# Overflow rounds moved ahead of the rounds of four, the last spread accumulated onto h in PSUM, and the final norm taken by token halves out of PSUM

## The chip, the cores and the metric

The kernel runs on one core of a Trainium2 chip. The metric is the device time of one execution in microseconds. Three executions of the kernel before took 942.13, 942.78 and 943.84 us; the median is 942.78.

## The reference

One layer of a streaming encoder over 512 tokens of width 1024, all float32. Two branches (a gMLP spatial gate and a sliding-window attention) are gated and merged onto the residual `h`. Then comes a mixture of 32 experts: each token picks one group of 8 experts and the two best in it. Last comes a norm of the sum:

```python
def hierarchical_moe(x, w_rg, b_rg, w_re, b_re, w_gate, w_up, w_down):
    ...
    for e in range(N_EXPERTS):
        h = jax.nn.silu(xf @ w_gate[e]) * (xf @ w_up[e])
        y = y + combine[:, e:e + 1] * (h @ w_down[e])
    ...
        h = h + hierarchical_moe(hn, ...)
    return rmsnorm(h, norm_final_g)
```

`w_gate` and `w_up` are 1024x512 per expert, `w_down` 512x1024: 6 MB an expert, 192 MB in all, each read once.

## The kernel before, in words

Up to about 450 us it computes the two branches and the router. The change touches only what follows, the expert stage and the end.

**Rounds.** The experts go through 14 rounds (`ITERS`). Rounds 0 to 11 take two experts each, with room for 64 tokens per expert. Rounds 12 and 13 take four each, the eight experts with the fewest tokens, with room for 32. Tokens that find no room go to overflow rounds, a loop at the end behind a branch on `n_over > 0`, on each of TensorE, ScalarE, VectorE and SyncE. With these inputs nothing overflows: no overflow round runs in the trace, and each engine jumps over the loop's body.

**A round on TensorE.** `project` gate into bank 0 (L734), `turn_weights` (L744: the rows' weights turned into bank 7), `project` up into bank 1, half 0 of the spread of the round before (L797, L798), `turn_rows` (L751), half 1 of that spread, `project_down` into banks 5 and 6 (L766). For the last round `project_last_down` (L782) takes the down weights in three parts as they land. The fp32 weights of two or four experts stand in column tiles of 64 or 32 of the array. `spread` multiplies a one-hot matrix with `y_hi` and `y_lo`, and brings each row of y to its token: eight sums of 128x512, one for each of four token tiles and two halves. Ahead of each even round `gather_rows` (L718) picks the tokens' rows of the normed h for two rounds, 64 matmuls, with a one-hot that VectorE makes in `make_onehot` (L1379 to L1395), and `copy_pack` moves them to SBUF.

**A round on the other engines.** ScalarE: silu, the copy of the turned rows (`actT`), `y_hi` (L1006). VectorE: `row_weights`, in odd rounds `make_onehot` for the next two, `act_on_rows` (L1472), `add_rows` of the round before (L1491: eight adds of a sum in PSUM onto `h_tok`), `low_y` (L1480). So a round's spread and adds lie inside the next round.

**The weights.** SyncE issues them in order (L351). A step is one matrix of two experts, 4 MB, issued as two DMAs of 2 MB. There are four slots of SBUF, and step k waits until TensorE has finished the projection of step k-4. In numbers: rounds 0 to 11 are steps 0 to 35. Round 12 has gate 36 and 37, up 38 and 39, down 40 and 41; round 13 has 42 to 47. So steps 40 and 41 are issued when gate 12 is done, 42 and 43 when up 12 is, 44 and 45 when down 12 is, 46 and 47 when gate 13 is. Step 47 comes in three parts (L419), and behind it `final_g` (L424).

**The end.** `spread` of round 13, `add_rows`, then each engine loads the count `n_over` and branches. VectorE takes bn statistics of token tiles 2 and 3, ScalarE squares of tiles 0 and 1, GpSimd multiplies tiles 2 and 3 with `final_g` (L472). VectorE computes the root for all four (`inverse_root`: Newton steps on 128x4 elements) and finishes tiles 0 and 1 (L1540), ScalarE scales tiles 2 and 3 (L1030), and SyncE stores four tiles of 512 KB (L438). Semaphores tie all this together; there is no planner, the order is that of the code of each engine.

Of the kernel before, what the change touches and what calls it, by code (L numbers as in the profile page):

```python
# [7 lines left out]
F32 = mybir.dt.float32  # L8
# [7 lines left out]
P = 128  # L16
# [6 lines left out]
def build_block(nc, x, norm_mix_g, w_in, gate_bias, gmlp_ln_g, gmlp_ln_b, gmlp_w_s, gmlp_b_s,  # L23
# [28 lines left out]
    LIGHT_ROWS = ROWS // 2  # L52
    HEAVY = SORTED - LIGHT
    ITERS = FIXED // 2 + HEAVY // 2 + LIGHT // 4
    OV_ROW = ITERS * P
    assert ITERS % 2 == OV_PAIRS % 4 == 0
# [72 lines left out]
    result = at("result", [P, TT, D], F32, 32)  # L129

# [47 lines left out]
    with ctx:  # L178
# [57 lines left out]
        for c in range(UNITS):  # L236
# [33 lines left out]
        row_step, onehot_ready = sem("row_step"), sem("onehot_ready")  # L270
        pack_done, pack_a, pack_b = sem("pack_done"), sem("pack_a"), sem("pack_b")
        gate_done, up_done, silu_ready, rows_ready, rows_turned, actT_ready = (
            sem(n) for n in ("gate_done", "up_done", "silu_ready", "rows_ready", "rows_turned", "actT_ready"))
        y_left, down_done, y_hi_ready, y_lo_ready = (sem(n) for n in ("y_left", "down_done", "y_hi_ready", "y_lo_ready"))
        weights_turned, row_weight_ready, onehotT_ready = (
            sem(n) for n in ("weights_turned", "row_weight_ready", "onehotT_ready"))
        spread_done, h_added = sem("spread_done"), sem("h_added")
        ysq_summed, final_gained, out_stored = sem("ysq_summed"), sem("final_gained"), sem("out_stored")
        y_rstd_ready = sem("y_rstd_ready")
# [4 lines left out]
        h_final = sem("h_final")  # L284
# [21 lines left out]
        SPREAD_BANKS = ((2, 3, 5, 6), (7, 0, 1, 2))  # L306


        def experts_of(i):
            return 4 if i >= (FIXED + HEAVY) // 2 else 2  # L310

# [12 lines left out]
        def over_slot(j, q, m):  # L324

            slot = (3 * q + m) % 4
            before = STEPS_DONE // 4 - (1 if slot == LAST_SLOT else 0)
            return [(slot, 32 * (before + 3 * j + (3 * q + m) // 4) + (64 if slot == 0 else 32))]
# [11 lines left out]
        def _(sp):  # L340
# [7 lines left out]
            def load_step(slot, w, e0, e1):  # L348

                for s, e in enumerate((e0, e1)):  # L350
                    sp.dma_start(R[2 * slot + s][:, :].rearrange("p (a n) -> p a n", a=1),  # L351
                                 w[0, bass.ds(e, 1), :, :].rearrange("a (p c) n -> p a (c n)", p=P)
                                 ).then_inc(slot_loaded[slot], 16)
# [34 lines left out]
            DONE = (gate_done, up_done, down_done)  # L388
            for i in range(1, ITERS):
                n_e, r = experts_of(i), 2 * i - FIXED  # L390
                if i < FIXED // 2:
# [7 lines left out]
                for m, w in enumerate((w_gate, w_up, w_down)):  # L399
                    if i == 1 and m == 0:  # L400
                        continue
                    for a in range(n_e // 2):
                        k = step_at[i, m, a]
                        i4, m4, _ = steps[k - 4]
                        if k == 4:
                            for half, done in enumerate((gate_half_done, gate_done)):
# [16 lines left out]
            sp.wait_ge(routed, 1)  # L423
            sp.dma_start(final_g[:, :], norm_final_g.partition_broadcast(P)).then_inc(late_loaded, 16)  # L424
            n_over = sp.value_load(ov_count[0:1, 0:1], min_val=0, max_val=OV_TILES)

            with sp.If(n_over > 0):
                with sp.Fori(0, OV_PAIRS // 4) as j:
                    for q in range(4):
                        k = 4 * j + q  # L430
                        e0 = sp.value_load(ov_expert[0:1, bass.ds(2 * k, 1)], min_val=0, max_val=NE - 1)
                        e1 = sp.value_load(ov_expert[0:1, bass.ds(2 * k + 1, 1)], min_val=0, max_val=NE - 1)
                        sp.wait_ge(down_done, 4 * j + ITERS + q)
                        for m, w in enumerate((w_gate, w_up, w_down)):
                            load_step((3 * q + m) % 4, w, e0, e1)
# [7 lines left out]
        def _(pool):  # L443
# [32 lines left out]
        def _(pe):  # L476
# [220 lines left out]
            def gather_first():  # L697

                for part, ready in ((hn_hi, hn_hi_ready), (hn_lo, hn_lo_ready)):
                    for t in range(TT):  # L700
# [3 lines left out]
                        for c in range(KT):  # L704
# [4 lines left out]
                            if last and c % 2 == 1:  # L709
                                mm.then_inc(pack_done, 1)  # L710

            def gather_rows(g):

                pe.wait_ge(onehot_ready, g)
                for c in range(KT):
# [5 lines left out]
                    if c % 2 == 1:  # L721
                        mm.then_inc(pack_done, 1)

            def project(slots, odd, dst, done, packed=None, half_done=None):

                for slot, loaded in slots:
                    pe.wait_ge(slot_loaded[slot], loaded)
                n_e = 2 * len(slots)
                w = P // n_e
                for c in range(KT):  # L730
                    if packed is not None and c % 2 == 0:
                        pe.wait_ge(pack_b if c // 2 % 2 else pack_a, packed + c // 4)
# [8 lines left out]
            def turn_weights(odd):  # L741
# [3 lines left out]
                mm.then_inc(weights_turned, 1)  # L745

            def turn_rows(i):

                pe.wait_ge(rows_ready, i + 1)
                for c in range(FT):  # L750
                    mm = pe.transpose(bank[4][:, c * P:(c + 1) * P], act_rows[:, c, :], ident[:, :])  # L751
                mm.then_inc(rows_turned, 1)

            def project_down(slots, i, added):

                pe.wait_ge(actT_ready, i + 1)
                for slot, loaded in slots:
                    pe.wait_ge(slot_loaded[slot], loaded)
# [806 lines left out]
```

## Time and profile before

| | us |
|---|---|
| median of three executions | 942.78 |
| profiled execution | 942.76 |
| its span | 941.0 |
| TensorE busy in the span | 860.6 |
| VectorE busy | 438.5 |
| ScalarE busy | 211.2 |
| GpSimd busy | 8.4 |

All times below are counted from the start of the span. Section 2 of the page cuts the span into 40 slices of 23.5 us; a digit is the busy share of a slice in tenths. A TensorE matmul in fp32 appears as two records in the trace, one of the rounded fp32 form as one. "idle before" in a timeline is the engine's idle time ahead of the row, and behind the arrow stands what ended it.

### The profile page before, as it was taken

The numbers are of one execution on the slowest core, as the hardware profiler recorded it, in microseconds if no ns is written. First come the engines' busy times: TensorE is split into PE (matmuls) and PEld (weight loads), VectorE is DVE, ScalarE is ACT, GpSimd is POOL, SyncE is SP. The second block draws the span as 40 slices with busy tenths as digits, with TensorE's granted clock in tenths as the row PEclk, the third lists the DMA queues.
The fourth block names the chain that finished last, engine by engine and source line by source line (L and its number), as shares of the span: only waits on it lengthen the run. The fifth ranks groups of instructions, "written<-read, shape, count | busy, mean of one in ns | idle before, by whom it ended". The sixth has DMA issues, their size and how long they took to land.

```text
span 941.0 us, 11130 instructions
## 1 busy us (share of the span) xinstructions
PE 860.6 (91%) x4569; PEld 558.1 (59%) x4569; DVE 438.5 (47%) x811; ACT 211.2 (22%) x369; POOL 8.4 (1%) x17
## 2 busy tenths in 40 slices
PE   2999999999999999999699999999999999984481
PEld 2888888877777888888534546445464454531131
DVE  3528416677675344446785144351443513512026
ACT  5422232464444222223110111001110011100001
POOL 0000000000000100000000000000000000000001
PEclk9999999999999999999799999999999999997696
DMA  8343222121222643782289999999999999999982
GB/s 313 90 90 90 91 88 90 45 91 59 77 90 56 198 135 90 292 377 90 90 357 418 400 428 431 409 430 415 429 426 416 425 419 427 428 414 431 426 353 91
DMA packets 64838, 247.37 MB, mean 263 GB/s; under 512 B 21872, under 2 KB 45456, under 8 KB 52240
## 3 DMA queue, kind: packets, MB, share of 16 engines
q1 hardware_dynamic: 64432, 246.59, 66.8%
q8 instruction: 38, 0.62, 0.3%
q14 instruction: 16, 0.13, 0.0%
q10 hardware_dynamic: 352, 0.02, 0.0%
HBM read 244.50 MB, written 2.10 MB: 262 GB/s over the span
## 4 chain that ended last, share of the span: by engine, by line
PE 85%; DMA 8%; DVE 3%; issue 2%; ACT 1%; SPq 1%; DVEq 0%; ACTq 0%
PE bank L734 20%; PE bank L495 10%; PE bank L497 10%; PE bank L496 10%; PE bank L766 9%; PE bank L718 4%; PE bank L522 3%; PE bank L523 3%; PE bank L524 3%; DMA R<-w_gate 3%; PE bank L797 2%; DMA R<-w_down 2%; PE bank L798 2%; DMA R<-w_up 2%; PE bank L559 1%
## 5 line engine op out<-in xcount | busy, mean ns | idle before, releaser
L734 PE MATMUL bank<-R,packT 128*64 128x512 f32 (+1 forms) x1024 | 204.1, 620 | 22.4 <-DMA R<-w_up 12.1
L734 PEld LDWEIGHTS bank<-R,packT 128*64 128x64 f32 (+1 forms) x1024 | 64.3, 134 | 146.1 <-issue 145.3
L1058 DVE TENSOR_TENSOR wlo<-raw,whi 128x2048 fp32r<-128x2048 f32 x34 | 77.8, 2287 | 93.3 <-ACT whi L861 93.3
L495 PE MATMUL bank<-xnT_hi,whi 128*128 128x512 f32 x288 | 113.6, 395 | 0.6 <-DVE wlo L1058 0.6
L497 PE MATMUL bank<-xnT_hi,wlo 128*128 128x512 f32 x288 | 112.2, 390 | 0.0
L496 PE MATMUL bank<-xnT_lo,whi 128*128 128x512 f32 x288 | 112.1, 389 | 0.0
L766 PE MATMUL bank<-R,actT 128*64 128x512 f32 (+1 forms) x448 | 96.1, 626 | 7.8 <-DMA R<-w_down 7.1
L861 ACT ACTIVATE whi<-raw 128x2048 fp32r<-128x2048 f32 x34 | 65.0, 1911 | 73.6 <-PE bank L497 38.7
L766 PEld LDWEIGHTS bank<-R,actT 128*64 128x64 f32 (+1 forms) x448 | 30.0, 138 | 67.0 <-issue 67.0
L1491 DVE TENSOR_TENSOR h_tok<-bank,h_tok 128x512 f32<-128x512 f32 x112 | 68.0, 676 | 1.0 <-PE bank L798 1.0
L495 PEld LDWEIGHTS bank<-xnT_hi,whi 128*128 128x128 f32 x288 | 54.1, 188 | 12.3 <-issue 1.4
L497 PEld LDWEIGHTS bank<-xnT_hi,wlo 128*128 128x128 f32 x288 | 54.0, 188 | 11.4
L496 PEld LDWEIGHTS bank<-xnT_lo,whi 128*128 128x128 f32 x288 | 54.1, 188 | 10.7
L1480 DVE SCALAR_TENSOR_TENSOR y_lo<-bank,small,y_hi 128x512 fp32r<-128x512 f32 x28 | 21.0, 751 | 82.6 <-ACT y_hi L1006 82.6
L1466 DVE TENSOR_REDUCE small<-bank 128x1 f32<-128x512 f32 x14 | 9.7, 691 | 96.4 <-PE bank L744 96.4
L797 PE MATMUL bank<-y_hi,onehotT 128*128 128x512 f32 x112 | 46.5, 416 | 1.7 <-DVE y_lo L1480 1.7
L718 PE MATMUL bank<-onehot,hn_hi 128*128 128x256 f32 x192 | 46.9, 286 | 0.0
L718 PE MATMUL bank<-onehot,hn_lo 128*128 128x256 f32 x192 | 46.2, 282 | 0.0
L1006 ACT ACTIVATE y_hi<-bank,small 128x512 fp32r<-128x512 f32 x28 | 19.3, 688 | 118.3 <-PE bank L766 108.8
L798 PE MATMUL bank<-y_lo,onehotT 128*128 128x512 f32 x112 | 44.0, 393 | 0.0
L1472 DVE TENSOR_TENSOR act_rows<-silu_g,bank 128x512 f32<-128x512 f32 x14 | 15.1, 1080 | 60.9 <-PE bank L734 60.9
L1001 ACT ACTIVATE actT<-bank 128x512 f32<-128x512 f32 x14 | 8.4, 599 | 147.6 <-PE bank L751 147.6
(255 smaller groups left out, 1144.5 us busy)
## 6 DMA issues: line engine op xcount, KB each, us to landing
R<-w_gate SPq DMA_DIRECT2D x32, 2048.0 KB, 13.5
R<-w_up SPq DMA_DIRECT2D x30, 2048.0 KB, 13.4
R<-w_down SPq DMA_DIRECT2D x30, 2048.0 KB, 15.4
raw<-w_in SPq DMA_DIRECT2D x18, 1024.0 KB, 5.1
raw<-w_in SPq DMA_DIRECT2D x16, 256.0 KB, 4.3
raw<-w_branch_a SPq DMA_DIRECT2D x4, 1024.0 KB, 5.1
raw<-w_branch_b SPq DMA_DIRECT2D x16, 256.0 KB, 4.4
raw<-w_out SPq DMA_DIRECT2D x4, 1024.0 KB, 7.6
```

What stands on the lines that cost most here:

```text
L495: pe.matmul(dst, hi_w, hi_x, start=start, stop=False)
L496: pe.matmul(dst, hi_w, lo_x, start=False, stop=False)
L497: return pe.matmul(dst, lo_w, hi_x, start=False, stop=stop)
L522: pe.matmul(dst, xT_hi[:, kk, ts], w_h[:, k, :], start=first, stop=False)
L718: mm = pe.matmul(bank[PACK_BANKS[c // 2]][:, (c % 2) * 2 * P:(c % 2 + 1) * 2 * P], part[:, t, c, :], onehot[:, t, :], start=(t == 0 and pa ...
L734: mm = pe.matmul(dst[s * w:(s + 1) * w, :], packT[:, c, odd * P + s * w:odd * P + (s + 1) * w], R[2 * slots[s // 2][0] + s % 2][:, c * DE: ...
L766: mm = pe.matmul(bank[5 + n][s * w:(s + 1) * w, :], actT[:, c, s * w:(s + 1) * w], R[2 * slots[s // 2][0] + s % 2][:, c * D + n * 512:c * ...
L797: pe.matmul(dst, onehotT[odd][:, t * P:(t + 1) * P], y_hi[:, n * 512:(n + 1) * 512], start=True, stop=False)
L798: pe.matmul(dst, onehotT[odd][:, t * P:(t + 1) * P], y_lo[:, n * 512:(n + 1) * 512], start=False, stop=True).then_inc(spread_done, 1)
L861: act.activation(whi[c % 2][:, :], raw[c % 2][:, :], ACT.Copy).then_inc(hi_split, 1)
L1058: dve.tensor_tensor(wlo[c % 2][:, :], raw[c % 2][:, :], whi[c % 2][:, :].bitcast(F32), ALU.subtract).then_inc(lo_split, 1)
L1491: dve.tensor_tensor(part, bank[SPREAD_BANKS[n][t]][:, :], part, ALU.add).then_inc(h_added, 1)
```

## The change

- The rounds are split into 12 rounds of two (`QUADS`) and the two rounds of four. Behind round 11 its spread and its adds are done at once, all engines load the count and branch, and the overflow rounds stand there. Their semaphores are a set of their own (`over`), beside those of the main rounds (`main`).
- `make_onehot` and `gather_rows` for rounds 12 and 13 come behind the branch. `row_both` is lowered by one instruction in place of two.
- SyncE loads `final_g`, the count, and branches ahead of the loads of round 12 (step 36).
- Round 12's spread and adds come right behind its down projection, and TensorE waits for all of them ahead of gate 13.
- For round 13 nothing is added onto `h_tok`. An identity matmul in fp32 puts each 128x512 part of `h_tok` into a PSUM bank (`start_final`), and the spread accumulates onto it (`spread_final`). The first six identity matmuls stand ahead of the last down projection, the other two (into banks 5 and 6, which hold y until then) between the spreads.
- The final norm works on these eight sums: ScalarE squares each out of PSUM; VectorE multiplies three with `final_g` while it waits; the root is taken once for tiles 0 and 1 and once for 2 and 3; VectorE finishes the other sums out of PSUM. ScalarE scales one half tile, GpSimd does nothing.

The core of the diff (the rest passes `line`, which is `main` or `over`, to the functions of a round):

```diff
+        FINAL = ((0, 0, 2), (0, 1, 3), (1, 0, 0), (1, 1, 7), (0, 2, 1), (1, 2, 4), (0, 3, 5), (1, 3, 6))
...
+            def load_overflow():
+                sp.wait_ge(routed, 1)
+                sp.dma_start(final_g[:, :], norm_final_g.partition_broadcast(P)).then_inc(late_loaded, 16)
+                n_over = sp.value_load(ov_count[0:1, 0:1], min_val=0, max_val=OV_TILES)
+                with sp.If(n_over > 0):
...
             for i in range(1, ITERS):
                 n_e, r = experts_of(i), 2 * i - FIXED
+                if i == QUADS:
+                    load_overflow()
...
-            for t in (0, 2, 1, 3):
-                sp.wait_ge(result_low if t < 2 else result_high, t % 2 + 1)
+            for t in range(TT):
+                sp.wait_ge(result_low, (1, 2, 4, 6)[t])
+                if t == 1:
+                    sp.wait_ge(result_high, 1)
                 sp.dma_start(out[0, t * P:(t + 1) * P, :], result[:, t, :]).then_inc(out_stored, 16)
...
-            pool.wait_ge(late_loaded, 16 * 6)
-            pool.wait_ge(h_final, 1)
-            for t in range(2, TT):
-                pool.tensor_tensor(result[:, t, :], h_tok[:, t, :], final_g[:, :], ALU.mult).then_inc(final_gained, 1)
...
+            def start_final(j):
+
+                n, t, b = FINAL[j]
+                pe.matmul(bank[b][:, :], ident[:, :], h_tok[:, t, n * 512:(n + 1) * 512], start=True, stop=False)
+
+            def spread_final(j):
+
+                n, t, b = FINAL[j]
+                pe.matmul(bank[b][:, :], onehotT[1][:, t * P:(t + 1) * P], y_hi[:, n * 512:(n + 1) * 512], start=False, stop=False)
+                pe.matmul(bank[b][:, :], onehotT[1][:, t * P:(t + 1) * P], y_lo[:, n * 512:(n + 1) * 512],
+                          start=False, stop=True).then_inc(last_spread, 1)
...
             for n in range(2):
-                spread(ITERS - 1, n, 1)
+                spread(main, QUADS - 1, n, 1)
+            pe.wait_ge(main.h_added, 8 * QUADS)
             n_over = pe.value_load(ov_count[0:1, 0:1], min_val=0, max_val=OV_TILES)
             with pe.If(n_over > 0):
...
+            gather_rows(main, QUADS // 2)
+            project(main, slots_of(QUADS, 0), 0, bank[0], main.gate_done, packed=QUADS + 1)
+            turn_weights(main, 0)
+            project(main, slots_of(QUADS, 1), 0, bank[1], main.up_done)
+            turn_rows(main, QUADS)
+            project_down(main, slots_of(QUADS, 2), QUADS, None)
+            for n in range(2):
+                spread(main, QUADS, n, 0)
+            last = QUADS + 1
+            pe.wait_ge(main.h_added, 8 * last)
+            project(main, slots_of(last, 0), 1, bank[0], main.gate_done)
+            turn_weights(main, 1)
+            start_final(0)
+            start_final(1)
+            pe.wait_ge(main.silu_ready, last + 1)
+            start_final(2)
+            pe.wait_ge(main.onehotT_ready, last + 1)
+            start_final(3)
+            project(main, slots_of(last, 1), 1, bank[1], main.up_done)
+            turn_rows(main, last)
+            start_final(4)
+            pe.wait_ge(main.actT_ready, last + 1)
+            start_final(5)
+            project_last_down(slots_of(last, 2), last)
+            pe.wait_ge(main.y_lo_ready, 2 * last + 1)
+            spread_final(0)
+            spread_final(1)
+            pe.wait_ge(main.y_lo_ready, 2 * last + 2)
+            spread_final(2)
+            spread_final(3)
+            start_final(6)
+            start_final(7)
+            for j in range(4, 8):
+                spread_final(j)
...
+            for j, (n, t, b) in enumerate(FINAL):
+                act.wait_ge(last_spread, j + 1)
+                act.activation(square_of[:, j, :], bank[b][:, :], ACT.Square, scale=float(D) ** -0.5,
+                               accum_out=half_sq[:, TT * n + t:TT * n + t + 1]).then_inc(ysq_summed, 1)
             act.wait_ge(y_rstd_ready, 1)
+            act.wait_ge(y_gained, 2)
+            act.activation(result[:, 1, 0:512], result[:, 1, 0:512], ACT.Copy, scale=rstd[:, 1:2]).then_inc(result_high, 1)
...
+            make_onehot(main, QUADS // 2, 13 * (QUADS // 2) + 3)
+            copy_pack(main, QUADS // 2)
+            for i in range(QUADS, ITERS):
+                row_weights(main, i, i % 2)
+                act_on_rows(main, i)
+                low_y(main, i, i % 2)
+                if i < ITERS - 1:
+                    add_rows(main, i)
...
             dve.wait_ge(late_loaded, 16 * 6)
+            for j in range(3):
+                gain_y(j)
+            final_rstd(0)
+            dve.wait_ge(y_gained, 3)
+            dve.tensor_scalar(result[:, 0, :], result[:, 0, :], rstd[:, 0:1], None, ALU.mult).then_inc(result_low, 1)
+            finish_y(3)
+            final_rstd(1)
+            for j in range(4, 8):
+                finish_y(j)
```

## Rows read from the trace of the kernel before

**Rows 1.** The page, section 2: busy share of the DMA engines, 40 slices.

```profile
DMA  8343222121222643782289999999999999999982
```

**Rows 2.** Table of stretches: length, busy us (count) by engine, PEclk, DMA share, GB/s.

```profile
646.00:706.00 60.00, 60.00 (x308) 28.60 (x308) 24.01 (x44) 6.34 (x10) 0.00 (x0) 1.00 1.00 423
```

**Rows 3.** Timeline of PE in rounds 12 and 13: start, us, instruction, idle before.

```profile
816.92 0.38 PE L718 MATMUL bank<-onehot,hn_hi 128*128 128x256 f32 x1
...
824.77 7.07 PE L734 MATMUL bank<-R,packT 128*32 128x512 f32 x64
...
835.46 8.77 PE L734 MATMUL bank<-R,packT 128*32 128x512 f32 x64 [3.02 <-DMA R<-w_up]
...
855.66 9.36 PE L766 MATMUL bank<-R,actT 128*32 128x512 f32 x64 [7.09 <-DMA R<-w_down]
875.13 9.86 PE L734 MATMUL bank<-R,packT 128*32 128x512 f32 x64 [10.11 <-DMA R<-w_gate]
...
894.69 8.62 PE L734 MATMUL bank<-R,packT 128*32 128x512 f32 x64 [9.11 <-DMA R<-w_up]
...
909.47 7.07 PE L782 MATMUL bank<-R,actT 128*32 128x512 f32 x64 [1.81 <-DMA R<-w_down]
```

**Rows 4.** Timeline of SP's DMA issues: start, us for all of the row.

```profile
791.36 7.70 SPq L351 DMA_DIRECT2D R<-w_gate  x4
805.68 12.16 SPq L351 DMA_DIRECT2D R<-w_up  x4
831.91 2.12 SPq L351 DMA_DIRECT2D R<-w_down  x4
844.42 2.89 SPq L351 DMA_DIRECT2D R<-w_gate  x4
...
888.94 3.18 SPq L424 DMA_DIRECT2D final_g<-norm_final_g  x1
```

**Rows 5.** Chain that ended last, in the tail: start, us, what.

```profile
916.59 1.49 DVE y_lo L1480 x2
...
919.02 4.89 DVE h_tok L1491 x8
...
923.94 0.54 DVEq L1511
...
924.90 0.56 issue
```

**Rows 6.** Timeline of DVE in rounds 11 and 12.

```profile
799.86 0.40 DVE L1379 TENSOR_SCALAR weight_a<-row_iota,small 128x256 f32<-128x256 f32 x1
...
804.40 0.69 DVE L1393 TENSOR_SCALAR onehot<-weight_a 128x1024 fp32r<-128x1024 f32 x1
...
817.76 0.75 DVE L1480 SCALAR_TENSOR_TENSOR y_lo<-bank,small,y_hi 128x512 fp32r<-128x512 f32 x1 [2.55 <-ACT y_hi L1006]
```

**Rows 7.** Chain that ended last, a whole gather.

```profile
757.34 7.86 PE bank L718 x64
```

**Rows 8.** Timeline of the tail, DVE and GpSimd (POOL).

```profile
925.67 4.66 POOL L472 TENSOR_TENSOR result<-h_tok,final_g 128x1024 f32<-128x1024 f32 x2 [614.74 <-DVE small L1524]
...
928.27 2.07 DVE L1533 TENSOR_TENSOR small<-small 128x2 f32<-128x2 f32 x1
...
930.78 0.17 DVE L1046 TENSOR_SCALAR small<-small 128x4 int32<-128x4 int32 x1
...
932.76 1.28 DVE L1540 SCALAR_TENSOR_TENSOR result<-h_tok,small,final_g 128x1024 f32<-128x1024 f32 x1
...
933.96 1.28 DVE L1540 SCALAR_TENSOR_TENSOR result<-h_tok,small,final_g 128x1024 f32<-128x1024 f32 x1
```

**Rows 9.** The four stores' line (L438), from issue to landing.

```profile
DMA to landing us min/median/max: 2.6/3.9/4.9
```

**Rows 10.** Timeline of ACT, a square of the router's norm.

```profile
430.42 0.63 ACT L956 ACTIVATE squares<-h_tok 128x512 f32<-128x512 f32 x1 [9.29 <-DVE h_tok L1232]
430.95 0.19 ACT L956 ACTIVATION_READ_ACCUMULATOR squares<-h_tok 128x1 f32 x1
```

More of the change, by code:

```diff
@@ L405, in _ @@
                         if k == 4:
-                            for half, done in enumerate((gate_half_done, gate_done)):
+                            for half, done in enumerate((gate_half_done, main.gate_done)):
                                 sp.wait_ge(done, 1)
@@ L1015, in _ @@
+            for i in range(QUADS):
+                expert_pair(main, i, i % 2)
+                if i % 2 and i < QUADS - 1:
+                    copy_pack(main, i // 2 + 1)
             n_over = act.value_load(ov_count[0:1, 0:1], min_val=0, max_val=OV_TILES)
             with act.If(n_over > 0):
-                with act.Fori(ITERS // 2, (ITERS + OV_PAIRS) // 2) as g:
-                    copy_pack(g)
+                with act.Fori(0, OV_PAIRS // 2) as g:
+                    copy_pack(over, g)
@@ L1493, in _ @@
-            copy_pack(0)
-            for i in range(ITERS):
+                        dve.tensor_tensor(part, bank[SPREAD_BANKS[n][t]][:, :], part, ALU.add).then_inc(line.h_added, 1)
+            copy_pack(main, 0)
+            for i in range(QUADS):
                 if i == 0:
@@ L1533, in _ @@
-            then(dve.tensor_tensor(mean_sq[:, 2:4], mean, mean, ALU.mult))
-            then(dve.tensor_tensor(mean_sq[:, 2:4], mean_sq[:, 2:4], var, ALU.add))
-            dve.wait_ge(ysq_summed, 2)
-            inverse_root(rstd, mean_sq)
-            dve.memset(root_work, 0.0).then_inc(y_rstd_ready, 1)
-            dve.wait_ge(late_loaded, 16 * 6)
-            for t in range(2):
-                dve.scalar_tensor_tensor(out=result[:, t, :], in0=h_tok[:, t, :], scalar=rstd[:, t:t + 1],
-                                         in1=final_g[:, :], op0=ALU.mult, op1=ALU.mult).then_inc(result_low, 1)
+                dve.tensor_scalar(row_both, row_both, -2.0 * P, None, ALU.add).then_inc(over.row_step, 1)
@@ new lines, in _ @@
+                dve.wait_ge(over.row_step, 1)
+                dve.memset(root_work, 0.0).then_inc(over_pair_free, 1)
+                with dve.Fori(0, OV_PAIRS // 2) as g:
+                    make_onehot(over, g + 1, 13 * g + 1)
+                    copy_pack(over, g)
+                    for odd in range(2):
+                        o = 2 * g + odd
+                        row_weights(over, o, odd)
+                        act_on_rows(over, o)
+                        low_y(over, o, odd)
+                        add_rows(over, o)
+                        dve.wait_ge(over.h_added, 8 * o + 8)
+                        dve.memset(root_work, 0.0).then_inc(over_pair_free, 1)
@@ new lines, in _ @@
+                dve.tensor_scalar(row_both, row_both, float(2 * P * (1 + OV_PAIRS // 2)), None, ALU.add).then_inc(over.row_step, 1)
+                dve.wait_ge(over.row_step, 13 * (OV_PAIRS // 2) + 2)
+            make_onehot(main, QUADS // 2, 13 * (QUADS // 2) + 3)
+            copy_pack(main, QUADS // 2)
+            for i in range(QUADS, ITERS):
+                row_weights(main, i, i % 2)
+                act_on_rows(main, i)
+                low_y(main, i, i % 2)
+                if i < ITERS - 1:
+                    add_rows(main, i)
@@ new lines, in gain_y, with final_rstd @@
+            def gain_y(j):
+                n, t, b = FINAL[j]
+                dve.wait_ge(ysq_summed, j + 1)
+                dve.tensor_tensor(result[:, t, n * 512:(n + 1) * 512], bank[b][:, :], final_g[:, n * 512:(n + 1) * 512],
+                                  ALU.mult).then_inc(y_gained, 1)
+            def final_rstd(pair):
+                part = slice(2 * pair, 2 * pair + 2)
+                dve.wait_ge(ysq_summed, 4 * pair + 4)
+                then(dve.scalar_tensor_tensor(out=mean_sq[:, part], in0=half_sq[:, part], scalar=EPS,
+                                              in1=half_sq[:, TT + 2 * pair:TT + 2 * pair + 2], op0=ALU.add, op1=ALU.add))
+                inverse_root(rstd[:, part], mean_sq[:, part], biased=True)
+                dve.memset(root_work, 0.0).then_inc(y_rstd_ready, 1)
```

310 lines of the change are left out of this document (137 added, 173 removed).

## The prediction

> **What bounds the kernel now.** I read the page's strip first. From 55% of the span on, the row of the DMA engines stands at 9 tenths until the last slices [rows 1]: the stage that streams the experts' weights. The table of stretches says how full it is: DMA share 1.00 at 423 GB/s, with PE busy 60.00 of 60 us in the same stretch [rows 2]. PE and the weight stream are in step there; in the rounds of four PE falls back and the stream alone sets the pace. The PE timeline shows that: it waits 3.02, 7.09, 10.11, 9.11 and 1.81 us, each time for a weight DMA [rows 3].
>
> The SP timeline explains why the stream never stops [rows 4]. A load is issued when PE has finished the step that used the slot. The last two loads of round 12's up weights go out by 817.8 and land at 835.4, so work is queued until then. The next four issues come at 831.91, when gate 12 is done: 3.5 us before the stream would run dry. That 3.5 us is all the slack that the stream has in this place.
>
> After the last weights (PE's last stretch starts at 909.47) comes a serial tail to 941.0, which the chain of waits shows [rows 5]: y, spread, eight adds onto h, the branch, statistics, root, gain, store.
>
> **Part 1: the cut before the rounds of four.** Before, gather 12 ran straight behind down 11, from 816.92 to 824.77 [rows 3], because its onehot had been made in DVE time at 799.86 to 805.09 that no one waited for [rows 6], and spread 11 was laid into round 12. Now all of this stands in one line, since the overflow branch must see a finished h:
> - Down 11 ends at about 817.0 as before; y_lo of it at 817.76+0.75 = 818.5 [rows 6].
> - Spread 11 and its adds. In the tail of before the same pair of steps took from the end of y_lo (916.59+1.49 = 918.08) to 919.02+4.89 = 923.91, 5.83 us [rows 5]. So h stands at 824.4.
> - DVE loads the count and branches: from 923.94 to the next instruction at 925.46, 1.5 us [rows 5]. PE and ACT do it at the same time. 825.9.
> - make_onehot, now waited for: 804.40+0.69-799.86 = 5.2 us [rows 6]. The merged row_both instruction comes after the release. 831.1.
> - The gather of 64 matmuls: 7.86 us at full clock [rows 7]. PE has then been idle since the spread's end at about 822.5, 8.6 us. After idle times of 10.11, 9.11 and 7.09 us the next 64 matmuls took 9.86, 8.62 and 9.36 us instead of the 7.07 of a run without a stop [rows 3]: 1.6 to 2.8 us more. I take 2.2 (bounds 0 and 2.8): 841.2.
> - Gate 12: 7.07 us. Done at 848.3, against 831.9 before.
>
> So PE is 16.4 us late. What does the stream make of it? final_g is now issued ahead of round 12's loads, in SP's wait ahead of 791.36; its 3.18 us of issue [rows 4] and SP's own count load fit in it. The transfer, 512 KB, takes 1.2 us of the queue (two steps, 8 MB, land every 19.5 us [rows 3]: 875.13-855.66), and moves the end of the queued work from 835.4 to 836.6. The next issue is at 848.4. Its first bytes need some 1.4 us: the shortest store of 512 KB took 2.6 us [rows 9], less 1.2 of transfer. Idle stream: 849.8-836.6 = 13.2 us. Down 12's weights are in at 849.8+19.5 = 869.3, 13.7 us later than 855.6.
>
> Is any of it won back? The stream is saturated again from there: up 12 runs at once (its weights have long landed), ends near 856 and releases the next two loads; down 12 ends near 878.7, and 44/45 are issued behind a full queue; the second new wait, PE at `h_added` before gate 13, ends 0.8+0.8+5.8 later, about 886.2, and gate 13's weights land at 888.8. That cut is hidden by 2.6 us. The identity matmuls 0 to 5 stand where PE waits for up 13 (9.11 us) or for silu and act_rows. Each costs 0.88 us: eight matmul rounds of four column tiles took 7.07 us [rows 3], and this is one tile as wide as all. Four before up 13 are 3.5 us, seven at half clock, still within 9.11. All stays in the stream's shade, so the last down starts **13.7 us later** (bounds 10.5 and 17: gather at full clock and no start-up time, against a slow gather and a slower restart).
>
> **Part 2: the tail**, in the times of before, to be compared with the last result at 933.96+1.28 = 935.24 [rows 8]:
> - The spread of half 0 now waits for the first y_lo only: 917.34, start 917.5; first sum released 0.7 later, 918.2; four by 919.6 (0.455 each).
> - Two identity matmuls into the banks of y, 1.76 us (bounds: 3.5 at half clock, 0.9 if one costs 0.44), then four more pairs: the fifth sum at 921.7, the last at 923.1.
> - ACT squares one half after the other. One in the router's norm takes 0.63 plus the accumulator's 0.19, overlapped: 0.72 [rows 10], with its wait 0.75. Four by 921.25, eight by 924.8.
> - DVE: three gains of 0.7 beside the squares. Root of tokens 0 and 1: eleven small steps at 0.2 (ten took 930.78 to 932.76 [rows 8]), 921.3 to 923.5. Scale of row 0 0.8, half 3 0.7: 925.0. Second root: 927.2. Four finishes at 0.61 (as the adds, eight in 4.89): 929.7.
> - So the last result is 5.5 us earlier. The store: the first three are issued at 924.3, 925.4 and 928.5 and don't queue ahead of the last, so it ends 0.1+2.6 to 3.9+0.3 behind, 3.5 [rows 9], where before 941.0-935.24 = 5.8 passed with four in a row. 2.3 us more.
>
> The tail gains **7.5 us** (bounds 5.5 and 8.5). What goes is clear from the rows: eight adds of 4.89, the branch of 1.5, and one step of 2 elements that takes 2.07 us [rows 8].
>
> That step ends at 930.34, and GpSimd's two products end at 925.67+4.66 = 930.33 [rows 8]: DVE stood behind them. The Trainium skill, "SBUF — State Buffer", "SBUF: two separate sides", says that DVE and GpSimd share a port pair under an exclusive lock. The trace agrees. If it were not so and the stall came from something that stays, the tail would gain 5.4 us.
>
> **Sum.** Span 941.0+13.7-7.5 = 947.2. The profiled execution took 942.76 for a span of 941.0, and the median of three is 942.78, so 1.8 is added: **949.0 us**. With the bounds crossed: 10.5-8.5 = +2.0 gives 944.8, 17-5.5 = +11.5 gives 954.3.
>
> **Rivals.**
> A. *The jump over the overflow body stalls.* The body on PE is over 400 matmuls long; PE now jumps it with work behind it. The one jump that the trace shows with work behind it, DVE's, lost 0.56 us [rows 5], with an idle DMA. PE jumps at 825.4 and is wanted at 831.2, so 5.8 us are hidden. If the code came only when the queued weights are through, at 836.6, gather would start 5.4 us late, and DVE, if it stalled likewise, 10.7 us: 954.4 to 959.7. The Trainium skill, "Runtime: NRT & Kernel Launch", "Instruction fetch mechanics", states that a taken branch out of the prefetched window makes the engine fetch by DMA before it goes on. No run here shows how long that takes under a full stream.
> B. *The other side: the cut is free.* If the stream carried the hole, because gate 12 were done before 835.2 (the end of the queued work, 836.6, less 1.4 of start-up), only the tail would count: 942.8-7.5 = 935.3, faster. Against it: the line above would have to be 13.1 us shorter, and even with no gather slowdown and no branch it is 3.7 us shorter. For it: only that PE waits 31 us in all in the rounds of four [rows 3]; but it waits there for the stream, which is not slack of the stream.
> C. *The cut is paid in part.* A hole of 4 to 9 us, from a cause that I don't see (the stream running faster after a pause, say): 939.5 to 944.7.
>
> **How the numbers follow.** Forecast (944.8 to 954.3) 0.74; A 0.11, B 0.08, C 0.07. A measurement here tells 0.2% (1.9 us) from no change, so "same" is 940.9 to 944.7. Faster: B and a little of C, 0.10. Same: most of C, 0.05. Slower: 0.85. The range takes in the forecast's bounds and the lower part of A: 944.5 to 956.
>
> **What would show it.** Right: the SP timeline has the four issues of round 12's down weights near 848 instead of 831.91; a stretch of about 12 us around 837 to 850 with DMA near zero; PE idle about 8.6 us before the gather, which runs longer than 7.86; gate 13 still waiting for a DMA and not for h_added; the last down starting near 923; no GpSimd in the tail, and from the last down's end to the span's end 7.5 us less than now. Wrong: the issues of 831.91 staying where they are (B), the gather starting well after onehot is ready (A), or gate 13 waiting for the adds, which would make the second cut costly too.

## The result and the profile after

Four executions of the changed kernel took 951.21 to 952.0 us, median 951.6; before took 942.97 (four runs). The ratio is 1.0091 with a 95% interval of 1.0074 to 1.0109: slower by 8.6 us. The forecast was 949.0 and slower, its range 944.5 to 956. The profiled execution took 951.78 us over a span of 950.0.

The page's strips show one new thing: the 36th of the 40 slices (831.3 to 855.0 us) has a 3 where DMA stood at 9, and 146 GB/s between two slices above 400.

```profile
DMA  8343322122123634873299999999999999939993
GB/s 310 89 89 89 104 73 89 45 90 89 45 89 89 192 104 102 344 306 114 110 377 431 399 428 428 409 429 415 428 427 414 429 417 417 429 146 430 427 422 148
```

The table of stretches (length, busy us by engine with count, PEclk, DMA share, GB/s) answers to [rows 2]. The rounds of two are unchanged; the hole lies between 834 and 851, where the stream moved 41 GB/s and TensorE worked without a stop:

```profile
646.00:706.00 60.00, 60.00 (x307) 28.69 (x308) 23.89 (x43) 6.34 (x10) 0.00 (x0) 1.00 1.00 422
...
817.12:834.00 16.88, 5.58 (x24) 4.59 (x25) 10.78 (x23) 0.69 (x1) 0.00 (x0) 0.78 1.00 426
834.00:851.00 17.00, 17.00 (x142) 10.78 (x145) 2.61 (x4) 1.79 (x3) 0.00 (x0) 0.92 0.13 41
851.00:872.98 21.98, 6.40 (x60) 1.99 (x53) 1.09 (x2) 0.60 (x1) 0.00 (x0) 0.72 1.00 424
```

SyncE's issues, as in [rows 4]. The loads of down 12 go out at 849.21 instead of 831.91; final_g's own issue is at 780.84:

```profile
780.84 0.42 SPq L390 DMA_DIRECT2D final_g<-norm_final_g  x1
791.47 7.71 SPq L351 DMA_DIRECT2D R<-w_gate  x4
805.80 12.16 SPq L351 DMA_DIRECT2D R<-w_up  x4
849.21 2.05 SPq L351 DMA_DIRECT2D R<-w_down  x4
856.95 2.34 SPq L351 DMA_DIRECT2D R<-w_gate  x4
```

The chain before round 12, spread 11 to gate 12. It was not there before the change: in its place stood the 7.86 us of the gather alone.

```profile
819.58 4.89 DVE h_tok L1533 x8
824.49 0.55 DVEq L1556
...
830.54 0.70 DVE onehot L1438
831.25 1.09 issue
832.33 9.81 PE bank L719 x64
842.15 7.00 PE bank L735 x64
```

TensorE's timeline, as in [rows 3]. The waits ahead of gate 13, up 13 and the last down are still for a DMA, and these three start 17.4 us later than before, down 12 17.3:

```profile
842.08 7.07 PE L735 MATMUL bank<-R,packT 128*32 128x512 f32 x64
...
872.98 9.35 PE L767 MATMUL bank<-R,actT 128*32 128x512 f32 x64 [14.37 <-DMA R<-w_down]
...
892.57 9.79 PE L735 MATMUL bank<-R,packT 128*32 128x512 f32 x64 [4.68 <-DMA R<-w_gate]
...
912.13 8.55 PE L735 MATMUL bank<-R,packT 128*32 128x512 f32 x64 [5.75 <-DMA R<-w_up]
...
926.90 7.08 PE L781 MATMUL bank<-R,actT 128*32 128x512 f32 x64 [2.54 <-DMA R<-w_down]
```

So the delay is 926.90-909.47 = 17.4 us. The tail from there to the span's end took 941.0-909.47 = 31.5 us before and takes 950.0-926.90 = 23.1 now: 8.4 us gained. 17.4-8.4 = 9.0 is the difference of the two spans.

VectorE's timeline in the tail, as in [rows 8]: the gains run beside the squares, the first root ends at 940.66, and the last results are out at 946.91, 20.0 us behind the last down's start, against 935.24-909.47 = 25.8.

```profile
936.75 1.89 DVE L1586 TENSOR_TENSOR result<-bank,final_g 128x512 f32<-128x512 f32 x3 [1.24 <-ACT square_of L1070]
...
940.71 0.75 DVE L1608 TENSOR_SCALAR result<-result,small 128x1024 f32<-128x1024 f32 x1
...
944.85 2.06 DVE L1599 SCALAR_TENSOR_TENSOR result<-bank,small,final_g 128x512 f32<-128x512 f32 x3
```

### The profile page after: what moved, and what is told of

Its sections match the earlier page's. It is cut to its first block, busy times and chain, and to the rows that moved or that the text cites. A ratio compares the mean times of both kernels' runs of the same rounds, so it can differ in the third digit from the quotient of the medians.

```text
span 950.0 us, 11161 instructions
## 1 busy us (share of the span) xinstructions
PE 868.3 (91%) x4585; PEld 562.3 (59%) x4585; DVE 433.8 (46%) x807; ACT 212.2 (22%) x380; POOL 3.7 (0%) x15
## 4 chain that ended last, share of the span: by engine, by line
PE 86%; DMA 7%; DVE 4%; issue 2%; ACT 1%; SPq 1%; DVEq 0%; ACTq 0%
PE bank L735 20%; PE bank L496 10%; PE bank L498 10%; PE bank L497 10%; PE bank L767 9%; PE bank L719 5%; DMA R<-w_gate 4%; PE bank L523 3%; PE bank L524 3%; PE bank L525 3%; PE bank L796 2%; DMA R<-w_down 2%; PE bank L797 2%; PE bank L560 1%; DMA x_tok<-x 1%
## 5 line engine op out<-in xcount | busy, mean ns | idle before, releaser
L1533 DVE TENSOR_TENSOR h_tok<-bank,h_tok 128x512 f32<-128x512 f32 x104 | 63.2, 677 | 1.8 <-PE bank L797 1.8
L719 PEld LDWEIGHTS bank<-onehot,hn_hi 128*128 128x128 f32 x192 | 38.1, 199 | 14.1 <-issue 14.1
L796 PE MATMUL bank<-y_hi,onehotT 128*128 128x512 f32 x104 | 43.1, 414 | 3.3 <-DVE y_lo L1524 3.3
L797 PE MATMUL bank<-y_lo,onehotT 128*128 128x512 f32 x104 | 40.8, 392 | 0.0
```

The costliest lines, as they stand in the source:

```text
L719: mm = pe.matmul(bank[PACK_BANKS[c // 2]][:, (c % 2) * 2 * P:(c % 2 + 1) * 2 * P], part[:, t, c, :], onehot[:, t, :], start=(t == 0 and pa ...
L796: pe.matmul(dst, onehotT[odd][:, t * P:(t + 1) * P], y_hi[:, n * 512:(n + 1) * 512], start=True, stop=False)
L797: pe.matmul(dst, onehotT[odd][:, t * P:(t + 1) * P], y_lo[:, n * 512:(n + 1) * 512], start=False, stop=True).then_inc(line.spread_done, 1)
L1533: dve.tensor_tensor(part, bank[SPREAD_BANKS[n][t]][:, :], part, ALU.add).then_inc(line.h_added, 1)
```

## The experiments

Medians, each beside the kernel before on the same chip:

| run | us | before | ratio, 95% interval |
|---|---|---|---|
| changed kernel | 951.6 | 942.97 | 1.0091, 1.0074 to 1.0109 |
| tail only | 934.42 | 943.59 | 0.9903, 0.9887 to 0.9918 |
| cut only | 960.74 | 943.59 | 1.0183, 1.0169 to 1.0197 |
| rounds between 12 and 13 | 936.67 | 943.59 | 0.9928, 0.9915 to 0.9942 |
| early onehot | 949.91 | 943.59 | 1.0063, 1.0049 to 1.0077 |
| no branch | 949.0 | 944.06 | 1.0056, 1.0039 to 1.0073 |
| no branch, kept at work | 947.4 | 944.06 | 1.0038, 1.0024 to 1.0052 |
| early onehot, short body | 949.73 | 944.06 | 1.0059, 1.0042 to 1.0076 |
| jump in the tail | 937.06 | 944.06 | 0.9931, 0.9915 to 0.9948 |
| between, early jump | 934.93 | 943.53 | 0.9919, 0.9907 to 0.9932 |
| between, early jump, kept at work | 936.45 | 943.53 | 0.9924, 0.9911 to 0.9937 |
| between, final_g early | 936.87 | 943.53 | 0.9930, 0.9916 to 0.9944 |
| before without GpSimd's products | 941.89 | 943.53 | 0.9982, 0.9973 to 0.9991 |

### Each half alone

Tail only: the loops of all engines run on through round 12 as before the change, no overflow code.

```diff
-            for i in range(QUADS):
+            for i in range(QUADS + 1):
...
-            n_over = pe.value_load(ov_count[0:1, 0:1], min_val=0, max_val=OV_TILES)
-            with pe.If(n_over > 0):
-                ...
-            gather_rows(main, QUADS // 2)
```

> The changed kernel with the overflow branch and its rounds left out on every engine (they do nothing with these inputs, so the output is the same here), rounds 11 and 12 interleaved as before the change, and final_g again behind the last weights. Theory (two independent terms: a hole in the weight stream before round 12, and a shorter tail): only the tail's gain is left. From the last down projection's start to the span's end it took 31.53 us before and 23.10 after, so 942.97 - 8.4 = 934.5. Rival (the two terms are not independent: the tail profits from the late, rested stream or from the identity matmuls having room): gain of 4 to 6 only, 937 to 939. No hole at 835 to 850; the last down starts at 909.5.

Cut only: the changed kernel with the old end (`spread`, `add_rows`, statistics, GpSimd).

```diff
-            pe.wait_ge(main.y_lo_ready, 2 * last + 1)
-            spread_final(0)
-            ...
+            for n in range(2):
+                spread(main, last, n, 1)
```

> The changed kernel with the end of the kernel before: spread 13 into fresh banks, adds onto h, statistics, GpSimd's products; the cut before round 12 stays. Theory: the hole alone costs what the last down's start moved, 926.90 - 909.47 = 17.4, so 960.4. Rival (part of the delay comes with the identity matmuls or the new end of round 13): 955 to 958.

Measured: 934.42 and 960.74, that is -9.2 and +17.2 us. Their sum is +8.0, the change gave +8.6. Within the intervals (about 1.5 us on each side) the two halves add up, and all the loss is the cut's. In the tail-only trace the last down starts at 910.05.

### Another place for the cut

The overflow rounds stand behind round 12; their body (not run) makes the state of rounds 12 and 13 again.

```diff
-                if i == QUADS:
+                if i == QUADS + 1:
                     load_overflow()
...
                with dve.Fori(0, OV_PAIRS // 2) as g:
                    ...
+                make_onehot(over, OV_PAIRS // 2 + 1, 13 * (OV_PAIRS // 2) + 1)
+                copy_pack(over, OV_PAIRS // 2)
```

> The overflow rounds stand between rounds 12 and 13 instead of 11 and 12; rounds 0 to 12 are interleaved as before the change, the new tail is kept, final_g behind the last weights; the overflow body (not run here) makes onehot, pack and weights of group 6 again at its end. Theory: a serial cut costs only what PE and SP are late with the next issue while the queue of loads runs dry. Between 12 and 13 PE waits 10.1 us for gate 13's weights, with two steps queued: down 12 ends at 865.0, adds at 872.4, count and branch by 874 to 874.6, weights in at 875.1. So the cut is free: 934.5 to 935.5. Rival (code fetch behind the jump costs each engine a fixed stall, whatever it waits for): 936 to 938. Rival (any cut costs): 945 or more.

936.67: 6.9 us faster than before and some 15 faster than the changed kernel, but 2.2 above the tail alone, where I had expected at most one. That is the time of the first rival. The place makes the cut nearly free; what is left goes with a late start of TensorE. VectorE's adds ended at 867.54+4.87 = 872.41, and TensorE began gate 13 at 880.13 with its weights there:

```profile
880.13 8.83 PE L735 MATMUL bank<-R,packT 128*32 128x512 f32 x64 [9.51 <-issue]
...
895.26 7.07 PE L735 MATMUL bank<-R,packT 128*32 128x512 f32 x64 [2.28 <-DMA R<-w_up]
...
910.47 8.77 PE L781 MATMUL bank<-R,actT 128*32 128x512 f32 x64 [4.46 <-DMA R<-w_down]
```

7.7 us for a load of the count and a jump. The stream took no harm (the last down starts 0.4 later than in the tail-only kernel), but the last down ran at the lower clock at first (granted clock 0.59 from 910.4 to 914.0, after 4.46 us without work; 1.00 in the tail-only kernel from 910.0 on, after 1.88) and took 8.77 instead of 7.07.

### The onehot out of the line

```diff
-                if i % 2 and i < QUADS - 1:
+                if i % 2:
                     make_onehot(main, i // 2 + 1, 13 * (i // 2 + 1) + 3)
```

> The changed kernel, but round 12's onehot and weights are made in round 11, as before the change (the overflow body, not run here, makes them again). Theory: the hole shrinks one to one with the serial line. The 5.2 us of make_onehot go; gather can start behind the branch at 825.5 to 826.5 instead of 832.3, 6 us earlier, and with PE idle for 3 to 4 us instead of 9.7 its 64 matmuls may take 7.9 instead of 9.8: gate 12 done 6 to 8 us earlier, 943.6 to 945.6. Rival (the code that PE jumps to arrives late; 832.33 was set by that and not by onehot at 831.24): gather stays near 831 to 832, 950 to 951.6.

The rival was right. The 5.2 us of VectorE's work went, and 1.7 us came of it by the medians, 2.3 by the ratios. In the traces only 0.46 us of that lies between the first add and gate 12's start (22.11 us here, 22.57 in the changed kernel). The chain has nothing between the adds and the gather but TensorE itself:

```profile
819.11 4.88 DVE h_tok L1534 x8
823.99 7.75 issue
831.74 9.48 PE bank L719 x64
841.22 7.00 PE bank L735 x64
```

So TensorE's load and jump take 7.75 us, and in the changed kernel VectorE's onehot had covered all but 1.09 of it (the "issue" row above, 831.25).

The fetch of the code is in the traces too. Their pages list a DMA queue of instructions, q8, with 38 packets of 16 KB; between two of them TensorE issues some 250 instructions, so they are its code. Here one of these packets is moved from 829.21 to 830.28, 5.2 us behind the adds' end, and the gather begins 1.46 us behind it. In the changed kernel the packet ends at 830.88 and the gather begins 1.45 us later, at 832.33: what released it was the code, not the onehot. In the kernel between 12 and 13 the packet ends at 878.55, 1.58 us ahead of gate 13.

### What the jump costs, and what it hangs on

No branch: count load, branch and body left out on all engines, the cut kept.

> The changed kernel without the count's load, the branch and the overflow rounds on all four engines (they do nothing with these inputs); the serial cut before round 12 stays. In the early-onehot run TensorE began the gather 7.75 us after the adds' end with nothing to wait for but its own count load and jump; here that is gone, but the gather still waits for VectorE's onehot. Theory: VectorE's 1.5 us go, so onehot is out at 829.7; TensorE's last 1.1 us of jump beyond onehot go too: gather at 829.8, gate 12 done 2.6 us earlier: 949.0. Rival (the wait was not the branch but something in the cut): 951.6.

Measured 949.0, as expected; against its own before it is +4.9, where the changed kernel is +8.6. That is 3.7 us less, somewhat more than the 2.6 expected, with an interval of 1.6 us on each side of either number. The chain is the better measure. Counted from the first add (818.60 here, 819.58 in the changed kernel), the onehot is out at 10.2 us instead of 11.7 and the gather begins at 10.3 instead of 12.75, 2.45 earlier:

```profile
818.60 4.89 DVE h_tok L1500 x8
...
828.07 0.70 DVE onehot L1405
828.77 0.14 issue
828.90 10.19 PE bank L708 x64
```

Short body: the early-onehot kernel with `for q in range(1)` in place of `range(4)` in TensorE's overflow body.

> The early-onehot kernel with TensorE's overflow body cut to a quarter (one pair in place of four per pass of the loop; with these inputs the body isn't run, so the output is the same). Theory (the 7.75 us are the fetch of code that lies far off, behind a body of some 1200 instructions): with a quarter of it the target is nearer; if it lies within what has been fetched already, the jump costs what VectorE's does, 1.5 us: gather at 825.5, and at an idle time of 3 us at full clock; gate 12 done near 840.5 instead of 848.3, total 942 to 944. Rival (any taken jump on TensorE costs 7 us): 949.9, gather at 831.7.

Nothing: 949.73, and the same chain with 6.88 us of issue ahead of the gather at 831.89. The code is fetched here too, in a packet that ends at 830.44. A quarter of the code between branch and target doesn't help.

Jump in the tail: tail only, with TensorE's load, branch and full body behind `project_last_down`.

> The tail-only kernel (934.4) with TensorE's count load, branch and full overflow body put behind the last down projection, where the weight stream has ended; no other engine branches. Theory (the fetch waits behind the queued weights): with idle DMA engines the jump is short, 1.5 to 3 us from the last matmul's issue at 917 to 918.5 to 920, against a spread that starts at 918.2 anyway: 934.5 to 936.5. Rival (the jump costs its 7 us whatever the DMA does): first spread at 924 to 925, 940.5 to 941.5.

With the weight stream over (37 GB/s between 914 and 916, none from 916 to 918) the first spread started at 918.59, 2.5 us behind the last matmul's end at 916.08; in the tail-only kernel that gap is 0.9:

```profile
909.01 7.07 PE L770 MATMUL bank<-R,actT 128*32 128x512 f32 x64 [1.20 <-DMA R<-w_down]
918.59 0.50 PE L797 MATMUL bank<-y_hi,onehotT 128*128 128x512 f32 x1 [2.51 <-DVE y_lo L1496]
```

So the jump cost some 1.7 us here. The profiled execution (935.16) is the fastest of four, which reach to 938.37 with a median of 937.06; against their own before the kernel is 2.2 us behind the tail-only one. The other executions may have had a longer jump.

The 2.5 us are not all of the load and the jump, since TensorE issues them while its last matmuls still run. The code's packet bounds them better. It began at 915.97, at most 2.0 us behind the landing of the last weights (913.95), for which TensorE had waited ahead of its last matmuls. Under the full stream, in six kernels, the same packet began 4.4 to 5.4 us behind the adds' end, for which TensorE had waited ahead of its load. The packet itself (1.1 to 1.2 us) and the step from its end to the first matmul (1.4 to 1.6) are alike. So the stretch ahead of the packet is what grows, by at least 2.3 us. The tail of before, where DMA is idle as well, has the packet at 921.66, at most 2.0 us behind the first add (ended at 919.7), for which the last part of the spread waits. How much of it is the load of the count and how much the fetch waiting for its turn, no row tells. One difference besides the stream is left: in those six kernels VectorE loads and branches in the same microseconds, and in these two tails no other engine does (VectorE in the tail of before from 923.94 on).

VectorE's own load and jump took 1.5 us under the full stream (adds' end 824.46, next instruction 825.99), as in the tail of before; why they don't stall isn't shown, and the short body on TensorE speaks against length alone. The Trainium skill, "Runtime: NRT & Kernel Launch", "Instruction fetch mechanics", says that a taken branch out of the prefetched window stalls for a DMA fetch of the target; TensorE's packets agree with it (829.21 to 830.28, then the gather at 831.74).

### The clock in the gather

No branch, and nine idle matmuls of 128x512 ahead of the gather:

```diff
+            for _ in range(3):
+                pe.matmul(bank[4][:, :], ident[:, :], packT[:, 0:2, :].rearrange("p c q -> p (c q)"), start=True, stop=True)
             pe.wait_ge(main.h_added, 8 * QUADS)
+            for _ in range(6):
+                pe.matmul(...)
             gather_rows(main, QUADS // 2)
```

> As the run without the branch, with nine idle fp32 matmuls of 128x512 (ident by packT into bank 4, read by no one) on TensorE between spread 11 and gather 12: three ahead of the wait for the adds, six behind it, 0.88 us each. Theory: the gather took 9.8 instead of 7.86 us only because of the clock after 9.7 us without work; kept at work it takes 7.9, and the hole shrinks by that: 1.9 us less than the run without the branch, 947.1. Rival (the hole is set elsewhere, the gather's pace is hidden): no difference.

947.4 against 949.0: 1.6 us. The gather took 7.67 us instead of 10.19 in the run without them, and began late, since six matmuls were one too many (11.6 us behind the first spread matmul instead of 11.1):

```profile
819.21 0.47 PE bank L785
...
825.70 5.15 PE bank L830 x12
830.85 7.67 PE bank L708 x64
```

(L830 holds the six; fp32 matmuls count twice.) The granted clock was 1.00 over this gather and 0.74 from 828.9 to 839.1 in the run without them, over the gather there. The clock term is real; it was worth 2.5 us in the gather, less the 0.5 that the surplus matmul cost. The times, 1.0038 with an interval up to 1.0052 against 1.0056 from 1.0039 on, lean the same way and would not tell it alone.

### The place between 12 and 13, improved

```diff
+                if i == QUADS:
+                    pe.wait_ge(routed, 1)
+                    n_over = pe.value_load(ov_count[0:1, 0:1], min_val=0, max_val=OV_TILES)
...
             last = QUADS + 1
-            pe.wait_ge(main.h_added, 8 * last)
-            n_over = pe.value_load(ov_count[0:1, 0:1], min_val=0, max_val=OV_TILES)
             with pe.If(n_over > 0):
+                pe.wait_ge(main.h_added, 8 * last)
...
+            pe.wait_ge(main.h_added, 8 * last)
             project(main, slots_of(last, 0), 1, bank[0], main.gate_done)
```

> The kernel with the overflow rounds between 12 and 13, but TensorE loads the count ahead of down 12 and jumps as soon as spread 12 is issued; it waits for the adds only ahead of gate 13 (in the overflow body, not run here, too). There, with the stream full, TensorE's jump took 7.7 us (adds' end 872.4, gate 13 at 880.13, its weights in at 875.1 to 875.5). Theory: the jump now begins 2.8 us earlier and lacks the 1 us of the load: gate 13 at 876.3 to 877.3. That takes 3 to 4 us off gate 13 and nothing off the stream, which never ran dry there; what is won in time depends on TensorE's clock in the last down alone: 0 to 1.7 us, 935 to 936.7. Rival (gate 13's start sets the end): 933 to 934.

934.93, the best version with its overflow rounds in place: 8.6 us faster than before by the medians (6.4 to 8.8 by the interval), and some 16 faster than the changed kernel. Gate 13 waits for its weights again, and up 13 and the last down follow as in the tail-only kernel:

```profile
875.25 9.40 PE L735 MATMUL bank<-R,packT 128*32 128x512 f32 x64 [5.00 <-DMA R<-w_gate]
...
894.83 9.86 PE L735 MATMUL bank<-R,packT 128*32 128x512 f32 x64 [6.15 <-DMA R<-w_up]
...
909.81 7.08 PE L781 MATMUL bank<-R,actT 128*32 128x512 f32 x64 [1.45 <-DMA R<-w_down]
```

Gate 13 came earlier than expected (875.25 for 876.3 to 877.3), since the jump was over before the weights were in: the code's packet was moved from 871.61 to 872.67, 1.4 us behind the end of the last spread matmul (870.26). The time lies at the lower edge of what was expected. The difference of 1.7 us to the version before it equals the last down's 8.77-7.08; in the two profiled executions, 2.3 us apart, the last down also begins 0.7 earlier. But the two intervals overlap (0.9907 to 0.9932 and 0.9915 to 0.9942), so that step is read from the traces, not from the times. The overflow rounds themselves were not run in any of these kernels.

The same with four idle matmuls ahead of the last down:

> As the run before, with four idle fp32 matmuls (ident by h_tok into bank 5, read by no one, 0.88 us each) between identity matmul 5 and the last down projection. In the kernel with the overflow rounds between 12 and 13 the last down began after 4.46 us without work and took 8.77 us, in the tail-only kernel after 1.88 us and took 7.07. Theory: that clock is the whole difference of 2.2 us between the two; kept at work TensorE takes 7.07, and the kernel takes what the tail-only one does: 934.4 (ratio to before 0.990). Rival (the branch costs on other engines): 936.

A miss: 936.45. The early jump had already brought the last down back to 7.08 us, so there was nothing to keep at work; the four matmuls ran from 908.31 and held the last down until 911.84, 2.0 us after the time at which the run without them had its weights.

```profile
908.31 3.60 PE L875 MATMUL bank<-h_tok,ident 128*128 128x512 f32 x8
911.84 7.07 PE L781 MATMUL bank<-R,actT 128*32 128x512 f32 x64
```

### The price of final_g

The kernel between 12 and 13 with the load of final_g ahead of gate 13.

> The kernel with the overflow rounds between 12 and 13 (936.67), but final_g (512 KB) loaded ahead of gate 13's weights, in place of behind the last weights. Theory: in a stream that never runs dry every byte ahead of the last weights counts, 1.2 us: 937.9. In the changed kernel the same load cost nothing only because a hole of 14 us came behind it. Rival (a load of this size is hidden): 936.7.

936.87 against 936.67 cannot tell 1.2 us from nothing. In the traces the last down starts at 912.91 instead of 910.47. Of these 2.4 us, 0.7 is an offset that stands before final_g is issued at 834.61 (gate 12 begins at 825.57 and 824.86). The other 1.7 came behind it, for 1.2 expected. The last down then takes 7.07 instead of 8.77, which hides it. Open by the times.

### GpSimd in the old tail

```diff
-                pool.tensor_tensor(result[:, t, :], h_tok[:, t, :], final_g[:, :], ALU.mult).then_inc(final_gained, 1)
...
-                act.wait_ge(final_gained, t - 1)
-                act.activation(result[:, t, :], result[:, t, :], ...
+                act.activation(result[:, t, :], h_tok[:, t, :], ...
```

> The kernel before, without GpSimd's two products with final_g in the tail; ScalarE scales h_tok itself, so token tiles 2 and 3 of the output lack the gain. Theory (VectorE's step of two elements at L1533, 2.07 us, waits for the port that GpSimd holds): it takes 0.2 us, and the tail is 1.9 us shorter: 941 to 942 where before is 943 to 944. Rival (the stall is the fetch of code or the like): L1533 stays at 2 us, no difference.

941.89 against 943.53, 1.6 us less. The step of two elements, 2.07 us in [rows 8], takes 0.16:

```profile
927.39 0.28 DVE L1527 BATCH_NORM_AGGREGATE small<-small 128x2 f32<-128x12 f32 x2
927.70 0.16 DVE L1530 TENSOR_TENSOR small<-small 128x2 f32<-128x2 f32 x1
```

## Why the prediction was right, and where its sum was off

**The mechanism** was right: a serial line before round 12 makes TensorE late, SyncE's issue late, and the weight stream runs dry, which nothing behind it gives back; the new tail gains less than that. The two halves alone confirm it.

**The line up to gate 12.** Predicted and measured: end of the adds 824.4 and 824.46; VectorE behind the branch 825.9 and 825.99; onehot 831.1 and 831.24; the gather 10.1 and 9.81 us. Only its start was late, 832.33 for 831.2. That is rival A in a small form: I had TensorE's jump hidden with 5.8 us to spare behind the adds' end plus its load, and it took 7.87 us in all, 1.09 more than the onehot covered. Gate 12 was done at 849.1 for 848.3.

**From the late issue to the late weights.** This is the term of the sum that was mis-sized: 13.7 predicted, 17.3 measured at down 12. From the issue to the landing of its two steps I took 1.4 us and then 19.5, the steady interval of two steps, 20.9 in all. Measured are 849.21 to 872.98, 23.8 us. The trace counts each load's landing 16 times, once for each DMA engine, and shows what was missing. The last of the four loads of 2 MB landed at 870.64 on the first engine, at 871.60 on the fifteenth and at 872.85 on the sixteenth. Up to the first, 21.4 us had passed since the issue: four loads at 4.9 us, and 1.9 of start where I had 1.4. The distance from the first to the last, 2.2 us, I had put at nothing.

The five other kernels that keep the cut before round 12 say the same: 21.4 to 21.5 us to the first engine, 0.8 to 2.2 from the first to the last, and 22.5 to 23.8 from the issue to TensorE's start. So the 16 engines run apart, and the slowest sets the landing. The others meanwhile move the loads issued behind (856.95): between 851.0 and 872.98 the stream moved 424 GB/s x 21.98 us = 9.3 MB, but the two steps are 8.4 MB. In a full stream this evens out, since the engines start a load as far apart as they end it: before, the last engine's landings around down 12 lie 4.9 us apart (850.52, 855.42, 860.31), as the first one's do. The hole's other end shows the distance as well. The last load ahead of it landed from 834.52 to 839.12 over the 16 engines, while the DMA share fell from 0.61 to 0.38 and 0.08 (834 to 837). Why one engine falls behind is open.

The sum of it: issue 0.8 later, start 0.5, distance of the engines 2.2, which leaves 0.1 of the 3.6 us.

**The second cut and the identity matmuls** cost nothing, as predicted: the adds of round 12 ended at 889.62, gate 13's weights came at 892.57, 2.95 us of margin for 2.6.

**The tail** gained 8.4 for 7.5, within its bounds. Its own parts, 5.5 and 2.3, add up to 7.8, so 0.3 of the miss is a slip in the sum, and the forecast should have read 948.7. Counted from the last down's start, the first root began at 11.6 us (11.8 predicted), and the last result was out 5.8 us earlier than before for the 5.5 predicted: the squares followed each other at 0.57 us, not 0.75. Behind the last result stand 950.0-946.91 = 3.1 us for the 3.5 predicted: the four stores, spread out from 941.48 to 946.9, landed in 2.7 to 3.2 us. The tail's surplus gain hid a quarter of the cut's surplus cost (0.9 of 3.7 us): the forecast was 2.6 us off where the cut's term alone was 3.7 off.

**Rival B** was wrong for the reason given, and the cut-only run prices it: +17.2. What B says holds at another place, between 12 and 13. Rival C (939.3 to 944.3 by its hole of 4 to 9 us) had a stream that runs faster after a pause; it ran at 424 GB/s from 851.0 to 872.98, as before the change (423).

## What to carry to other kernels

Where a stream of loads is the bound, a serial cut costs the time that its next issue comes late beyond the queued work, plus the start of the stream and the distance from its first engine to its last; put it where TensorE waits for that stream with loads already queued. A branch over code that isn't run is not free either: measure it under the load under which it will run, and issue it ahead of the wait, not behind it. And price the halves of a change apart: this one held a gain of 9 us and a loss of 17.

## What the runs showed of the hardware that I had not expected

- TensorE's load of the count and jump over an unused body took 6.9 to 7.75 us under a full weight stream (four kernels, two places). The packet with its code began 4.4 to 5.4 us after what released the load, and at most 2.0 us with the stream over; cutting the body to a quarter changed nothing.
- The 16 landings of one 2 MB load lay 0.8 to 2.2 us apart behind the hole, 4.6 us at the load ahead of it. When the first 8.4 MB behind the hole had landed on all, 9.3 MB had been moved.
- An instruction of two elements on VectorE took 2.07 us beside GpSimd's product and 0.16 without it.
- The issue of final_g took 3.18 us on SyncE behind the last weights [rows 4], 3.6 to 4.2 in five other kernels and 0.42 at the same place in the kernel between 12 and 13. The full queue alone doesn't explain it.
